# Three of 192 weight tiles brought as one transfer of 96 rows and four of 8 rows

## The chip, the cores and the metric

The kernel runs on one core of a Trainium2 chip. The metric is the device time of one execution in microseconds (us); the times given are medians of several runs.

## The reference

One layer of an encoder on 512 tokens of width 2048, float32: four token mixers with an input and an output projection, then a mixture of experts. What surrounds the change is the mixture: each token picks two of 32 experts, and each expert is a gated MLP.

```python
expert = grp[:, None] * EXPERTS_PER_GROUP + top_i        # 2 of 32 experts a token
a = jax.nn.silu(xblk @ w_gate[e]) * (xblk @ w_up[e])     # (2048 x 768) each
return a @ w_down[e]                                      # (768 x 2048)
```

The three weight matrices of 32 experts are 604 MB in float32. They are read once, and the kernel brings all of them whatever the routing is.

## The kernel before

The first 560 us or so are the mixers, the projections and the router. Then PE (TensorE) goes through the 32 experts, two at a time (`PAIRS`), each on up to 64 gathered token rows.

An expert's weights come as six tiles (`PARTS`) of 128 partitions x 24,576 bytes, 3072 KB each: two of `w_gate`, two of `w_up`, two of `w_down`. There are 192 tiles (`TILES`), numbered by `n`; tile `n` is part `n % 6` of expert `n // 6`, except at the very end, where `TAIL` changes the order. They go through a ring of five slots (and a sixth for the first round; `RING`, `slot_of`), in the regions `region_rest`, `region_h` and `region_w`. Every tile but the last two is one DMA issued by SP in `weight` (L392 for gate and up, L394 for down). Tiles 190 and 191 are cut into five pieces (`LAST`, L442).

The order of the transfers is SP's program order, one queue. In the loop over `n`, SP waits for `tile_used`, which PE raises when it is through with a tile, and issues the next tile into the slot that came free:

```python
for n in range(RING + 1, TILES):
    sp.wait_ge(tile_used, n - RING if n <= 2 * RING else n - RING + 1)
```

So four to five tiles are with the DMA engines at any time. PE waits in `landed(n)` (L1225 to L1228) for tile `n`'s semaphore to have counted 16 more, and then runs `gate_up` (matmuls of L1202) or `down` (L1220). For the last expert the down projections are L1163 and L1176, with L1152 adding the results into the tokens (L1141 for the experts before). Once in two experts POOL issues a gather of token rows (L549), which uses the DMA engines too. SP's queue carries nothing else in this part but the tiles (and `final_norm` once).

A tile's transfer of 128 rows runs on the core's 16 DMA engines, eight rows to each.

Of the kernel before, what the change touches and what calls it, by code (L numbers as in the profile page):

```python
# [30 lines left out]
P = 128  # L31
# [35 lines left out]
QK = KT // 2  # L67
DK = FT // 2
PARTS = 6
# [11 lines left out]

def added(c, t):
    return ADDS.index((c, t)) + 1


def nth_tile(n):
    return divmod(n, PARTS) if n < TILES - 2 * PARTS else TAIL[n - (TILES - 2 * PARTS)]
# [8 lines left out]
def build(nc, x, mix_norm, w_in, w_fourier, w_spatial, b_spatial, conv_w, w_pool, pool_scale, out_norm,  # L96
# [3 lines left out]
    with ctx:  # L100
        def sem(name):
            return ctx.enter_context(nc.semaphore(name))
# [98 lines left out]
        ring_gu = [r.rearrange("p (a b) -> p a b", a=QK) for r in ring]  # L201
# [45 lines left out]
        def slot_of(n):  # L247
            return n if n <= RING else (n - RING - 1) % RING
# [12 lines left out]
        wg_v = w_gate[0].rearrange("e (p k) n -> e p k n", k=KT)  # L261
# [14 lines left out]
        final_landed = sem("final_landed")  # L276
        tile_landed = [sem(f"tile_landed{s}") for s in range(RING + 1)]
        last_landed = [sem(f"last_landed{k}") for k in range(len(LAST))]
        last_down, last_hi, last_lo = sem("last_down"), sem("last_hi"), sem("last_lo")
        last_sum, last_added, f_redone, f_pre = sem("last_sum"), sem("last_added"), sem("f_redone"), sem("f_pre")  # L280
        over_landed = [sem(f"over_landed{s}") for s in range(PARTS)]
# [49 lines left out]
        def _(sp):  # L331
# [56 lines left out]
            def weight(expert, part, slot, landed):  # L388
                if part < 4:
                    src = (wg_v, wu_v)[part // 2]  # L390
                    q = part % 2
                    sp.dma_start(ring_gu[slot], src[expert, :, q * QK:(q + 1) * QK, :]).then_inc(landed, 16)  # L392
                else:
                    sp.dma_start(ring_down[slot], wdn_v[expert, part - 4]).then_inc(landed, 16)  # L394

            def tile(n):
                s = slot_of(n)
                weight(*nth_tile(n), s, tile_landed[s])

            def save_columns(n):  # L400
# [6 lines left out]
            for u in (37, 38):  # L407
                raw_unit(u)
            sp.wait_ge(y_normed, KT)
            tile(0)  # L410
            for u in (39, 40):
                raw_unit(u)
# [3 lines left out]
            save_columns(2)  # L416
            sp.wait_ge(w_ready, UNITS)
            tile(1)

            def save_last(t):  # L420
# [3 lines left out]
            for t in range(NT - 1):  # L424
                save_last(t)
            sp.wait_ge(w_used, UNITS)
            tile(2)
            save_last(NT - 1)
            tile(3)
# [45 lines left out]
        def _(pool):  # L475
# [94 lines left out]
            for t in range(NT):  # L570
                pool.wait_ge(last_added, added(0, t))
                g.tensor_tensor(gained[:, t, :], x_sb[:, t, 0:FINAL], final_row[:, 0:FINAL], ALU.mult).then_inc(f_gained, 1)
# [3 lines left out]
        def _(ae):  # L576
# [173 lines left out]
            for t in (0, 1):  # L750
                ae.wait_ge(last_added, added(0, t))
                square_first(t, f_pre, 2 * t + 1)
# [13 lines left out]
            def rms_last(t):  # L766
                ae.wait_ge(last_added, max(added(0, t), added(1, t)))
                if t < NT - 1:
                    src, junk_t, pre = x_sb[:, t, HALF:], junk3[3 + t], stat[:, 16 + t:17 + t]
                else:  # L770
                    src, junk_t, pre = x_sb[:, t, :], junk4, eps
                a.activation(junk_t, src, ACT.Square, accum_out=stat[:, t:t + 1]).then_inc(f_sq, 1)
                ae.wait_ge(f_sq, t + 1)
                a.activation(stat[:, NT + t:NT + t + 1], stat[:, t:t + 1], ACT.Sqrt, bias=pre, scale=1.0 / D).then_inc(f_rms, 1)
# [19 lines left out]
        def _(pe):  # L794
# [361 lines left out]
            def down_early():  # L1156
                for q in (0, 1):
                    slot = landed(TILES - 4 + q)
                    for kk in range(DK):
                        for c in (0, 1):  # L1160
                            for n in (0, 1):
                                j = 2 * c + n
                                mm = t_.matmul(ps[n * SLOTS:(n + 1) * SLOTS, 6 + c, :], aT[:, kk, q * SLOTS:(q + 1) * SLOTS],  # L1163
                                               ring_down[slot][:, kk, j * 512:(j + 1) * 512],
                                               start=(q == 0 and kk == 0), stop=(q == 1 and kk == DK - 1))
                    mm.then_inc(tile_used, 1)
# [58 lines left out]
            def landed(n):  # L1225
                s = slot_of(n)
                pe.wait_ge(tile_landed[s], 16 if n <= RING else 16 * ((n - 1) // RING + 1))
                return s  # L1228

            plan(0, True)  # L1230
# [2 lines left out]
            for e in range(E):  # L1233
                i, b = divmod(e, 2)
                n = e * PARTS if e < E - 1 else TILES - 8
                if e == E - 1:
                    pe.wait_ge(at_ready, e)
                for part in range(4):
                    if part < 2:
                        pe.wait_ge(hte_ready, 2 * e + part + 1)  # L1240
                    gate_up(part, landed(n + part))
                    if i and part in ((0, 1) if b else (1, 2)):
                        pe.wait_ge(hte_ready, 2 * e + 2)
                        combine(i - 1, 2 * b + (part if b else part - 1))
                if i:
                    pe.wait_ge(comb_added, 8 * (i - 1) + 4 * b + 4)
                if not b:
                    if i + 1 < PAIRS:
                        plan(i + 1)
                    transpose_rows(i, 1)  # L1250
                elif i + 1 < PAIRS:
                    transpose_rows(i + 1, 0)
                transpose_act(e)
                if e < E - 2:
                    pe.wait_ge(at_ready, e + 1)
                    if e:
                        pe.wait_ge(m_lo_ready, 2 * e)
                    for part in (4, 5):
                        down(b, part, landed(n + part))
# [574 lines left out]
```

## Time and profile before

| | |
|---|---|
| median of 3 runs | 2025.66 us (2024.97 to 2026.42) |
| the profiled execution, its own time | 2022.0 us |
| its span, first to last instruction | 2020.2 us |
| PE busy | 1854.8 us, 92% |
| DVE, POOL, ACT busy | 595.2, 249.6, 182.8 us |
| HBM read | 679.73 MB |

The page's slices are a fortieth of the span each, 50.5 us. A digit of the DMA line is the mean busy share of the 16 DMA engines in tenths; the line of GB/s is what they moved. In the chain that ended last, "DMA" is time in which PE waited, directly or through others, for a transfer to land, counted from its issue.

### The profile page before, as it was taken

The page shows a single profiled execution, that of the slowest core. Times are in us where ns is not written, and L with a number is a line of the kernel's source. Part 1 is how long each engine was busy: PE and PEld are TensorE (multiplying, and loading weights), DVE is VectorE, ACT ScalarE, POOL GpSimd, SP SyncE. Part 2 cuts the span into 40 slices and gives each one's busy share as a digit, 9 for nine tenths or more (in the row PEclk, how much of TensorE's full clock was granted, in tenths as well). Part 3 has the DMA queues.
Part 4 walks back from the last instruction along what each step waited for, and adds up shares of the span by engine and source line. Part 5 has one row for each costly group of instructions (what it writes and reads, how often), then busy time and mean ns, then how long its engine had stood idle before and what let it go on. Part 6 is the DMA issues. An engine that isn't in the chain of part 4 may idle for free.

```text
span 2020.2 us, 20896 instructions
## 1 busy us (share of the span) xinstructions
PE 1854.8 (92%) x9414; PEld 1056.3 (52%) x9414; DVE 595.2 (29%) x839; ACT 182.8 (9%) x274; POOL 249.6 (12%) x100
## 2 busy tenths in 40 slices
PE   8999999999969999899889989999898989888895
PEld 7887878788844444444344444444344444434342
DVE  3221656621142223122222223222222313222224
ACT  4000110101110010000000000000001000000003
POOL 4333535444200000000000000000000000000001
PEclk9999999999979999999999999999999999999998
DMA  7222233443389999999999999999999999999995
GB/s 275 84 78 84 64 103 90 175 171 113 115 343 424 429 430 429 429 429 429 430 430 430 429 430 430 429 429 428 432 428 431 429 428 429 429 430 429 429 427 205
DMA packets 68746, 681.12 MB, mean 337 GB/s; under 512 B 10352, under 2 KB 13616, under 8 KB 42416
## 3 DMA queue, kind: packets, MB, share of 16 engines
q1 hardware_dynamic: 65792, 671.16, 79.7%
q0 software_dynamic: 2304, 8.39, 1.0%
q8 instruction: 76, 1.25, 0.3%
q10 hardware_dynamic: 560, 0.21, 0.0%
q14 instruction: 14, 0.11, 0.0%
HBM read 679.73 MB, written 8.39 MB: 341 GB/s over the span
## 4 chain that ended last, share of the span: by engine, by line
PE 55%; DMA 43%; DVE 1%; issue 0%; ACT 0%; DVEq 0%; ACTq 0%
DMA region_rest<-in_w_gate 23%; PE banks L1202 19%; PE banks L814 15%; PE banks L1008 9%; DMA region_w<-in_w_gate 8%; DMA region_rest<-in_w_up 5%; DMA region_h<-in_w_gate 5%; PE banks L1141 3%; PE banks L1220 2%; DMA region_w<-in_w_down 1%; PE banks L892 1%; PE banks L904 1%; PE banks L841 1%; PE banks L1126 1%; PE banks L1176 1%; DMA region_h<-x_rows,region_rest 1%
## 5 line engine op out<-in xcount | busy, mean ns | idle before, releaser
L1202 PE MATMUL banks<-region_rest,region_w 128*64 128x384 f32 x2464 | 425.3, 499 | 58.8 <-DMA region_rest<-in_w_gate 43.8
L1202 PEld LDWEIGHTS banks<-region_rest,region_w 128*64 128x64 f32 x2464 | 185.7, 140 | 289.9 <-issue 219.7
L1658 DVE TENSOR_TENSOR region_x<-banks,region_x 128x1024 f32<-128x1024 f32 x120 | 141.4, 1220 | 587.7 <-PE banks L1141 587.7
L814 PE MATMUL banks<-split_h,split_w 128*128 128x512 f32 x864 | 273.7, 394 | 0.5 <-DVE split_w L1310 0.5
L494 POOL TENSOR_TENSOR split_w<-region_rest,split_w 128x2048 fp32r<-128x2048 f32 x42 | 196.9, 4688 | 302.8 <-DVE split_w L1317 302.8
L1220 PE MATMUL banks<-region_rest,region_w 128*64 128x512 f32 x864 | 213.0, 650 | 15.8 <-DVE region_w L1684 12.4
L814 PEld LDWEIGHTS banks<-split_h,split_w 128*128 128x128 f32 x864 | 162.2, 188 | 35.2 <-issue 0.7
L549 POOL DMA_INDIRECT region_h<-x_rows,region_rest x16 | 16.0, 1001 | 1271.2 <-PE banks L1126 1260.1
L814 PE MATMUL banks<-split_w 128*128 128x512 f32 x432 | 168.2, 389 | 0.0
L1008 PE MATMUL banks<-split_w,split_h 128*128 128x512 f32 x512 | 159.2, 392 | 0.0
L1202 PE MATMUL banks<-region_w 128*64 128x384 f32 x832 | 141.5, 493 | 18.8 <-DMA region_w<-in_w_gate 16.0
L1202 PE MATMUL banks<-region_h,region_w 128*64 128x384 f32 x800 | 136.0, 493 | 14.9 <-DMA region_h<-in_w_gate 9.5
L1220 PEld LDWEIGHTS banks<-region_rest,region_w 128*64 128x64 f32 x864 | 64.8, 149 | 150.8 <-issue 125.7
L1664 DVE TENSOR_TENSOR split_w<-banks,split_w 64x1024 fp32r<-64x1024 f32 x60 | 73.2, 1220 | 184.7 <-ACT split_w L709 183.8
L1141 PE MATMUL banks<-split_w 128*128 128x512 f32 x480 | 126.6, 406 | 0.0
L1317 DVE CAST split_w<-region_rest 128x2048 fp32r<-128x2048 f32 x43 | 53.2, 1237 | 210.0 <-PE banks L814 118.5
L1141 PEld LDWEIGHTS banks<-split_w 128*128 128x128 f32 x480 | 85.4, 188 | 51.6 <-issue 35.9
L1202 PEld LDWEIGHTS banks<-region_w 128*64 128x64 f32 x832 | 62.2, 138 | 94.9 <-issue 71.0
L1008 PEld LDWEIGHTS banks<-split_w,split_h 128*128 128x128 f32 x512 | 95.4, 188 | 22.5 <-issue 3.1
L1202 PEld LDWEIGHTS banks<-region_h,region_w 128*64 128x64 f32 x800 | 59.3, 138 | 88.8 <-issue 66.4
L715 ACT ACTIVATE region_w<-banks,region_rest 128x384 f32<-128x384 f32 x32 | 18.6, 582 | 902.9 <-PE banks L1202 902.9
L1008 PE MATMUL banks<-split_w 128*128 128x512 f32 x256 | 99.7, 389 | 0.0
(236 smaller groups left out, 1255.7 us busy)
## 6 DMA issues: line engine op xcount, KB each, us to landing
region_rest<-in_w_gate SPq DMA_DIRECT2D x39, 3072.0 KB, 31.7
region_rest<-in_w_up SPq DMA_DIRECT2D x38, 3072.0 KB, 30.4
region_rest<-in_w_down SPq DMA_DIRECT2D x36, 3072.0 KB, 30.8
region_h<-in_w_up SPq DMA_DIRECT2D x13, 3072.0 KB, 30.8
region_w<-in_w_up SPq DMA_DIRECT2D x13, 3072.0 KB, 30.2
region_w<-in_w_down SPq DMA_DIRECT2D x13, 3072.0 KB, 31.1
region_w<-in_w_gate SPq DMA_DIRECT2D x13, 3072.0 KB, 31.1
region_h<-in_w_down SPq DMA_DIRECT2D x13, 3072.0 KB, 31.3
```

The lines of the kernel that those rows point to most:

```text
L494: g.tensor_tensor(w_lo[u % 2], raw[u % RAW], w_hi[u % 2].bitcast(F32), ALU.subtract).then_inc(w_ready, 1)
L814: mm = t_.matmul(ps[:, 4 * (c % 2) + m, :], w[s][:, kk, cols_m], h[:, k, :], start=(k == 0 and w is w_hi and h is h_hi), stop=(k == KT - 1 ...
L841: mm = t_.matmul(ps[:, m, :], w[0][:, kk, m * P:(m + 1) * P], h[:, kk, :], start=(kk == 0 and w is w_hi and h is h_hi), stop=False)
L892: mm = t_.matmul(half, ab[:, s, h, c * HD:(c + 1) * HD], dft[:, c, s, :], start=(c == 0 and a == 0), stop=(c == 1 and a == 1))
L904: mm = t_.matmul(ps[:, m, :], wf[:, k, m * P:(m + 1) * P], fT[:, k, :], start=(k == 0), stop=(k == NH - 1))
L1008: mm = t_.matmul(ps[:, 4 * ((n + 1) % 2) + t, :], y[:, k, rows_t], w[s][:, kk, :], start=(k == 0 and y is y_hi and w is w_hi), stop=(k == ...
L1141: mm = t_.matmul(ps[:, 2 + 2 * c + n, :], back[c][:, t * P:(t + 1) * P], y[c][:, n * 512:(n + 1) * 512], start=(y is m_hi), stop=(y is m_lo))
L1202: mm = t_.matmul(ps[h * SLOTS:(h + 1) * SLOTS, u, 0:HF], hTe[:, k, :], ring_gu[slot][:, kk, h * HF:(h + 1) * HF], start=(k == 0), stop=(k ...
L1220: mm = t_.matmul(ps[g * SLOTS:(g + 1) * SLOTS, 6 + n, :], aT[:, kk, q * SLOTS:(q + 1) * SLOTS], ring_down[slot][:, kk, (2 * c + n) * 512:( ...
L1317: v.tensor_copy(w_hi[u % 2], raw[u % RAW]).then_inc(w_hi_ready, 1)
L1658: v.tensor_tensor(tile, ps[:, 2 + 2 * c:4 + 2 * c, :], tile, ALU.add).then_inc(comb_added, 1)
L1664: v.tensor_tensor(y_rows(m_lo, b, c), ps[g * SLOTS:(g + 1) * SLOTS, 6:8, :], y_rows(m_hi, b, c).bitcast(F32), ALU.subtract).then_inc(m_lo_ ...
```

## The change

```diff
+EVEN = (36, 96, 156)
...
+        rest_landed = sem("rest_landed")
...
             def tile(n):
                 s = slot_of(n)
+                if n in EVEN:
+                    sp.dma_start(ring_gu[s][0:96], wg_v[n // PARTS, 0:96, 0:QK, :]).then_inc(tile_landed[s], 16)
+                    for r in range(96, P, 8):
+                        sp.dma_start(ring_gu[s][r:r + 8], wg_v[n // PARTS, r:r + 8, 0:QK, :]).then_inc(rest_landed, 16)
+                    return
                 weight(*nth_tile(n), s, tile_landed[s])
...
             def landed(n):
                 s = slot_of(n)
                 pe.wait_ge(tile_landed[s], 16 if n <= RING else 16 * ((n - 1) // RING + 1))
+                if n in EVEN:
+                    pe.wait_ge(rest_landed, 64 * (EVEN.index(n) + 1))
                 return s
```

Tiles 36, 96 and 156 are the first gate tiles of experts 6, 16 and 26. In the changed kernel each is issued as five DMAs: rows 0 to 95 on the tile's own semaphore, then rows 96 to 103, 104 to 111, 112 to 119 and 120 to 127 on a semaphore of their own, for which PE also waits. The 96 rows are six rows for each of 16 engines. The transfers of eight rows are meant for eight of the engines, one row each, so that these eight have 6 + 4 = 10 rows of the tile and the other eight have six. The bytes, their source and their place in SBUF are the same.

SP's instructions at tile 36, before (the tile is the first of the two at the third row):

```order
L394 DMA region_rest<-in_w_down 128x6144 [waits tile_used]
L392 DMA region_rest<-in_w_gate 128x6144 [waits tile_used] x2
L392 DMA region_h<-in_w_up 128x6144 [waits tile_used]
```

and in the changed kernel, whose lines are numbered at least four higher:

```order
L398 DMA region_rest<-in_w_down 128x6144 [waits tile_used]
L403 DMA region_rest<-in_w_gate 96x6144 [waits tile_used]
L405 DMA region_rest<-in_w_gate 8x6144 x4
L396 DMA region_rest<-in_w_gate 128x6144 [waits tile_used]
L396 DMA region_h<-in_w_up 128x6144 [waits tile_used]
```

The one transfer has become five, with no wait between them; the order of the tiles has not moved. The rows at tiles 96 and 156 read alike.

## Rows read from the trace of the kernel before

**Rows 1.** The page: DMA busy tenths and GB/s in 40 slices.
```profile
DMA  7222233443389999999999999999999999999995
GB/s 275 84 78 84 64 103 90 175 171 113 115 343 424 429 430 429 429 429 429 430 430 430 429 430 430 429 429 428 432 428 431 429 428 429 429 430 429 429 427 205
```

**Rows 2.** Busy time by stretch (PE, PEld, DVE, ACT, POOL, PEclk, DMA share, GB/s).
```profile
700.00:800.00 100.00, 92.10 (x512) 43.32 (x510) 24.99 (x36) 5.24 (x6) 0.98 (x1) 1.00 1.00 429
1300.00:1400.00 100.00, 93.37 (x497) 44.07 (x493) 26.33 (x43) 5.24 (x6) 0.99 (x1) 0.95 1.01 430
1800.00:1900.00 100.00, 90.12 (x487) 42.45 (x485) 23.69 (x36) 5.24 (x6) 0.99 (x1) 0.97 1.00 429
```

**Rows 3.** Waits of PE, 600 to 1990 us (total us, times, longest).
```profile
PE banks L1202 <- DMA region_rest<-in_w_gate: 43.8, 24, 4.2
...
PE banks L1202 <- DMA region_w<-in_w_gate: 16.0, 9, 2.5
PE banks L1202 <- DMA region_rest<-in_w_up: 14.8, 11, 2.0
PE banks L1202 <- DMA region_h<-in_w_gate: 9.5, 7, 2.0
```

**Rows 4.** DMA issues by line: count, KB each, median us to landing.
```profile
region_rest<-in_w_gate SPq DMA_DIRECT2D x39, 3072.0 KB, 31.7
```

**Rows 5.** Timeline of SP, 792 to 812 us: the issue of tile 36 and the next.
```profile
801.40 8.23 SPq L392 DMA_DIRECT2D region_rest<-in_w_gate  x2
```

**Rows 6.** Timeline of PE at the first use of tiles 36 and 156.
```profile
833.55 7.08 PE L1202 MATMUL banks<-region_rest,region_w 128*64 128x384 f32 x32 [2.03 <-DMA region_rest<-in_w_gate]
...
1729.82 3.45 PE L1202 MATMUL banks<-region_rest,region_w 128*64 128x384 f32 x20 [2.03 <-DMA region_rest<-in_w_gate]
```

**Rows 7.** The chain that ended last, 1900 us to the end.
```profile
1946.32 29.73 DMA region_w<-in_w_down
1976.05 0.04 issue
1976.09 5.37 PE banks L1163 x24
1981.46 5.18 PE banks L1176 x23
...
1990.90 5.33 PE banks L1176 x24
```

**Rows 8.** Timeline of PE, 1969 to 1992 us.
```profile
1968.80 5.37 PE L1163 MATMUL banks<-region_h,region_w 128*64 128x512 f32 x24 [0.61 <-DMA region_h<-in_w_down]
1976.09 5.37 PE L1163 MATMUL banks<-region_w 128*64 128x512 f32 x24 [1.92 <-DMA region_w<-in_w_down]
```

**Rows 9.** Busy time by stretch at the end of the weights (columns as in rows 2).
```profile
1968.00:1976.00 8.00, 5.56 (x26) 1.96 (x24) 0.56 (x1) 0.00 (x0) 0.00 (x0) 1.00 1.00 411
1976.00:1980.00 4.00, 3.91 (x18) 1.35 (x20) 0.00 (x0) 0.00 (x0) 0.00 (x0) 1.00 0.94 358
1980.00:1984.00 4.00, 4.00 (x22) 1.42 (x20) 1.84 (x3) 2.15 (x4) 0.00 (x0) 1.00 0.58 237
1984.00:1988.00 4.00, 2.61 (x14) 0.59 (x10) 1.44 (x3) 1.18 (x2) 0.00 (x0) 1.00 0.51 209
1988.00:1992.00 4.00, 3.15 (x14) 1.91 (x16) 2.65 (x3) 0.70 (x1) 0.56 (x1) 1.00 0.23 92
```

**Rows 10.** DMA queues: packets, MB, share of 16 engines.
```profile
q1 hardware_dynamic: 65792, 671.16, 79.7%
q0 software_dynamic: 2304, 8.39, 1.0%
q8 instruction: 76, 1.25, 0.3%
```

## The prediction

> **What bounds the kernel now.** First the page's slices. From the thirteenth to the thirty-ninth, about 600 to 1970 us, the DMA digit is 9 and the rate stands at 424 to 432 GB/s [rows 1]. The stretches of 100 us say it more finely: DMA share 1.00, 429 or 430 GB/s, with PE busy 90 to 93% [rows 2]. So all 16 DMA engines work without a gap, and PE, though it looks full, waits for landings: 43.8 us on gate tiles in `region_rest` alone, never more than 4.2 us at once [rows 3]. A tile lands 31.7 us after its issue [rows 4], over four times the 7.33 us that its 3,145,728 bytes take at 429 GB/s, so the queue is four tiles deep and never runs dry.
>
> The time is then decided by the DMA engine that ends last. Every tile gives each of 16 engines eight rows of 24,576 bytes. One row takes an engine 7.33 / 8 = **0.917 us**; I call this a row time.
>
> Do all engines end together? They don't. The share is 1.00 until 1976, 0.94 until 1980, then 0.58, 0.51 and 0.23 in stretches of 4 us [rows 9]. A share near one half for 8 us is what it looks like when half of the engines have run out and the other half goes on. The bytes of these four stretches are 4 x (358 + 237 + 209 + 92) = 3584 KB; all engines together would need 8.4 us for them and be done at 1984.4 instead of about 1990.7. So the late half stands some 8 to 10 us behind the early half, the last engine of which stops at about 1983. Where the lag comes from is only partly seen: instruction fetches (76 packets) and gathers (8.39 MB) use the same engines and need not be even [rows 10].
>
> Last the chain at the end. PE waits for the down tile issued at 1946.32, which lands at 1976.05, and runs on from there to the end with short steps of DVE and ACT [rows 7]. This is tile 189. Two tiles follow it, 14.7 us of work for each engine, so the late half brought its share of tile 189 at 1976.05 and the slowest of the early half at about 1983 - 14.7 = **1968.3**.
>
> **The change part by part.** *SP* issues twelve DMAs more. Tile 36 is issued at 801.40 and used at 833.55 [rows 5, 6]; a fraction of a microsecond on SP is hidden by that queue, so I count nothing. If the queue were empty it would cost that fraction, three times. *PE* waits on a second semaphore; it already waits 2.03 us for tile 36 and for tile 156 [rows 6], so the check itself is free, and only when the rows land matters.
>
> *The rows moved.* Three tiles with two rows less for one half and two more for the other: 6 row times, 5.5 us. If that is all, and the relieved half is the late one, tile 189 is complete in the late half at 1976.05 - 5.5 = 1970.5 and in the early half at 1968.3 + 5.5 = 1973.8. The later counts: 2.2 us earlier than now. PE can take this up, since it waits 1.92 us there and 0.61 us one step before [rows 8]. This part is **-2.2 us**, not 5.5, because the early half has a slow engine of its own. Its best bound is -5.5.
>
> *What the eight-row transfers do to each other.* In a tile of 128 rows each engine brings eight rows, and the 16 reach 429 GB/s: each writes at its full 26.8 GB/s, to partitions that no other engine writes in that tile. In the new transfers eight engines each write one row at the same time into eight neighbouring partitions, 96 to 103, then 104 to 111, and so on. The trace has no heavy transfer of this kind. Bounds: if neighbours don't disturb each other, one of these transfers takes one row time and there is no cost. If all eight share one way in that is as fast as one engine, it takes eight row times. In between, four engines on one way make four row times. I take the four, for two reasons: the rate of 26.8 GB/s for an engine is also what the whole machine shows divided by 16, so I see no spare speed on the way in; and the middle of one and eight in ratio is near three to four. The Trainium skill, page SBUF — State Buffer, section "Door 1: The DMA port swizzle", speaks against the change here: four neighbouring partitions share one port, and a transfer to partitions 0 to 3 got 27.6 GB/s in all; no run here has shown it yet, and by this rule one transfer of eight rows takes four row times or five, since a port also has its usual engine.
>
> With four, the four transfers of a tile take 16 row times where four were meant: 12 too many. They come one behind the other on each engine, so nothing overlaps. If the engine that regularly writes into those partitions takes its turn as well (five on a way), it is 20 and 16 too many. I take **13**, near the lower end, because the eight engines don't arrive at the same moment, which gives a little back. Three tiles: 39 row times, 35.8 us, all in the early half. It cannot be made up later: the engines have no gap [rows 2]. Nor can PE's spare 10% help, since it spares PE, not the DMA.
>
> *Sum.* Tile 189 in the early half: 1968.3 + 5.5 + 35.8 = 2009.6, against 1976.05 now: **+33.5 us**. What comes after it on PE is unchanged. On the profiled execution 2022.0 + 33.5 = 2055.5. The median of the runs shown is 3.7 us above that execution, so I forecast 2025.7 + 33.5 = **2059**. With 12 row times too many it is 2056, with 16 it is 2067; allowing for more give and take, the forecast's own range is 2048 to 2070. What is late next is the early half: it turns into the late one at tile 36, by 10 us or more.
>
> **The rivals.** *No disturbance.* Each engine writes at its own speed wherever it writes. Then only -2.2 us is left: 2023.5, between 2020 and 2025.7. For it: 16 transfers side by side reach 429 GB/s without a gap [rows 2], so engines don't trouble each other at HBM, and the 11 us of difference that the moved rows make is about the lag. Against it: nothing in the trace has two engines at neighbouring partitions for long. This is the case on the other side, not slower; it decides if an eight-row transfer takes under about 1.5 row times. A measurement of this kernel can tell 0.2%, 4.1 us, so it would mostly read as no change.
>
> *Two on a way.* The way in has twice an engine's speed, so four engines take two row times: four too many a tile, 12 in all, 11.0 us; 1968.3 + 5.5 + 11.0 - 1976.05 = +8.7: 2034.
>
> *All eight on one way.* 28 too many a tile, 84 in all, 77 us: +74.8, 2100. I see little for it, since a full tile's rows are neighbours across engines too and run at full rate.
>
> *The wrong half.* No view names an engine. If the eight engines that get ten rows are the late ones, without disturbance, they end 5.5 us later: 2031. The page DMA: Bandwidth & Descriptors of the Trainium skill, section "Why a DMA increments its semaphore by 16 and not by 1", has such a transfer on the lowest-numbered engines; which half lags no row here shows.
>
> *It doesn't do what it says.* The eight rows are spread over all 16 engines after all: no shift of load, no crowding worth the name, 2025.7.
>
> **How the numbers follow.** Four or five on a way 0.52; two on a way 0.10; eight 0.04; no disturbance 0.26, of which 0.06 gains over 4.1 us (the early half's slow engine is less slow than I read it) and 0.20 not; wrong half 0.05; no effect 0.03. Slower by over 0.2%: 0.52 + 0.10 + 0.04 + 0.05 = 0.71. Within: 0.20 + 0.03 = 0.23. Faster: 0.06. No disturbance has over 2 in 10, so the range has to reach it: from 2022.5, which leaves out the larger gains, to 2070, above the 2067 of the highest of the main case. It leaves out some 0.15.
>
> **What the profile of the changed kernel would show.** If I am right: PE's wait for tiles 36, 96 and 156 grows from 2.03 us to over 10, and "longest" on `in_w_gate` with it. The GB/s fall clearly below 429 in some 15 us before each of these landings, while the DMA share stays at 1.00: engines that are held up count as busy. The transfers of eight rows take some 15 us longer than the 96 rows from issue to landing. The end of the weights still shows a step in the DMA share, now with the other half first, and longer. If no disturbance: 429 GB/s throughout, waits of 2 to 3 us at the three tiles, and in the last 15 us of weights a DMA share that falls from 1.00 to 0 within about 5 us. If the wrong half: the same rate, but the stretch of half share is 5 to 11 us longer. I am wrong altogether if the time rises while both the rate and the half-share stretch stay as they are; then it would be SP or PE, which I put at nothing.

## The result, and the profile after

The changed kernel takes 2089.3 us (median of 4 runs, 2081.1 to 2095.8) against 2025.3 us before: ratio 1.0317, 95% interval 1.0302 to 1.0333, slower by 64 us. The forecast was slower, 2059 us, in a range that ended at 2070. The sign and the three places were right; the size, 33.5 us, was half of what came. The profiled execution took 2087.4 us, its span is 2085.6.

The page of the changed kernel, its DMA lines in 40 slices (52.1 us each now):

```profile
DMA  7222133443499999999999999999999999999993
GB/s 266 81 94 78 66 101 95 173 162 121 171 389 424 431 427 387 367 429 429 430 429 430 429 430 327 389 432 428 429 431 429 429 429 301 374 427 429 430 414 127
```

Against [rows 1]: the digit stays at 9 from the thirteenth slice to the thirty-ninth, the rate does not stay. It dips in three places (387 and 367, 327 and 389, 301 and 374), where tiles 36, 96 and 156 are in transfer. Elsewhere it stands at 424 to 432 as before, up to the thirty-ninth slice (414). The DMA engines are busy all through and move less.

The first of the three places in steps of 5 us (columns as in rows 2):

```profile
815.00:820.00 5.00, 4.55 (x33) 2.98 (x29) 1.03 (x2) 0.00 (x0) 0.00 (x0) 1.00 0.98 416
820.00:825.00 5.00, 4.80 (x24) 1.64 (x24) 1.34 (x3) 0.00 (x0) 0.00 (x0) 1.00 1.10 369
825.00:830.00 5.00, 1.47 (x6) 0.29 (x4) 0.00 (x0) 0.00 (x0) 0.00 (x0) 0.81 1.03 236
830.00:835.00 5.00, 5.00 (x14) 1.42 (x12) 0.00 (x0) 0.00 (x0) 0.00 (x0) 0.50 1.09 182
835.00:840.00 5.00, 2.36 (x12) 0.56 (x8) 1.50 (x2) 2.04 (x2) 0.00 (x0) 1.00 1.00 147
840.00:845.00 5.00, 0.00 (x0) 0.00 (x0) 0.94 (x1) 0.00 (x0) 0.00 (x0) 0.68 0.88 157
845.00:850.00 5.00, 2.13 (x8) 1.05 (x10) 0.00 (x0) 0.00 (x0) 0.00 (x0) 0.50 0.94 383
```

The DMA share stays near 1.00 while the rate falls to 147 GB/s. Against 429 these seven stretches lack 13 + 60 + 193 + 247 + 282 + 272 + 46 GB/s over 5 us each, 5565 KB, which is 13.0 us of transfer at the full rate. The trouble begins at 820 us, before the eight-row transfers run: tile 36 comes behind four others in the queue, its 96 rows come first, and the first of its eight-row pieces on any engine lands at 834.6 us. Most of the loss comes later, though: by the same view 315 GB/s from 815 to 833 us, 4.8 us lost, and 223 GB/s from 833 to 850 us, 8.2 us lost.

PE's waits, 600 to 2060 us, and its timeline at tile 36:

```profile
PE banks L1211 <- DMA region_rest<-in_w_gate: 66.3, 23, 10.6
PE banks L1229 <- DMA region_rest<-in_w_down: 26.1, 6, 10.9
```
```profile
829.10 8.26 PE L1229 MATMUL banks<-region_rest,region_w 128*64 128x512 f32 x24 [3.54 <-DMA region_rest<-in_w_down]
847.87 12.58 PE L1211 MATMUL banks<-region_rest,region_w 128*64 128x384 f32 x64 [10.51 <-DMA region_rest<-in_w_gate]
```

The first use of tile 36 is at 847.87 instead of 833.55 [rows 6], after a wait of 10.51 us. The tile before it, which the change doesn't touch, is also late (PE waits 3.54 us for it at L1229, the same matmuls as L1220 before). The longest wait for such a down tile, 10.9 us, comes at tile 96, again for the tile before the cut one. So the cut tile holds up its neighbours.

The end of the weights (columns as in rows 2), and the chain that ended last there:

```profile
2028.00:2032.00 4.00, 3.33 (x18) 1.41 (x18) 0.56 (x1) 0.00 (x0) 0.00 (x0) 1.00 0.90 370
2032.00:2036.00 4.00, 2.20 (x12) 0.55 (x7) 0.00 (x0) 0.00 (x0) 0.00 (x0) 1.00 0.35 137
2036.00:2040.00 4.00, 2.49 (x6) 0.77 (x8) 0.00 (x0) 0.00 (x0) 0.00 (x0) 0.56 0.94 322
2040.00:2044.00 4.00, 4.00 (x14) 1.23 (x12) 0.00 (x0) 0.00 (x0) 0.00 (x0) 0.59 0.34 137
2044.00:2048.00 4.00, 4.00 (x22) 1.26 (x18) 1.57 (x3) 2.15 (x4) 0.00 (x0) 1.00 0.12 48
2048.00:2052.00 4.00, 2.88 (x14) 0.70 (x10) 1.46 (x3) 1.05 (x2) 0.00 (x0) 1.00 0.06 26
```
```profile
2006.32 31.14 DMA region_w<-in_w_down
2037.46 0.04 issue
2037.51 8.22 PE banks L1172 x24
2045.72 5.18 PE banks L1185 x23
```

The step near one half for 8 us [rows 9] is gone. In its place most engines run dry by 2036, since SP's issue of the fourth of the five last pieces takes 14.0 us and that of the fifth begins only at 2035.7 (the reason is not shown), and one or two of 16 go on to 2052 (shares 0.12 and 0.06). Tile 189 lands at 2037.46 instead of 1976.05 [rows 7]: **61.4 us** later. From there to the end of the span it takes 48.1 us, before 44.2 us: **4.0 us** more, since PE had stood idle and its granted clock was 0.56 and 0.59 in these stretches, near the lower of its two levels, 1.2 of 2.4 GHz: the 24 matmuls of L1172 took 8.22 us instead of 5.37 (L1163 before), and after a second idle time, at 0.69, the 8 of L1161 took 3.40 instead of 2.06 (L1152 before). Together 65.4 us, the growth of the span.

The trace also holds each engine's own increment of a tile's semaphore. When the first and the last of the 16 engines had brought their share of a tile, in us, and how much later the last was than before:

```
tile      before            changed kernel        last engine
38        843.8 to  848.0    856.3 to  862.1       +14.0
98       1288.7 to 1296.0   1317.8 to 1331.0       +35.0
159      1741.2 to 1751.6   1792.6 to 1812.5       +60.9
189      1963.4 to 1976.0   2017.3 to 2037.5       +61.4
```

14, 21 and 26 us for the three cut tiles and next to nothing in between. The first engine is late nearly as much: 12.5, 29.2, 51.4 and 54.0 us. That the early half alone would be held up was wrong from the first tile on: all 16 are. Before, the 16 increments of tile 189 stand in two groups, eight from 1963.4 to 1968.1 and eight from 1974.2 to 1976.0, which bears out the two halves of the prediction. In the changed kernel 14 stand from 2017.3 to 2026.6 and the last two at 2033.0 and 2037.5: two engines decide the landing. The semaphore of the eight-row transfers also shows that they run on eight engines: each of the 12 has eight increments at its landing and one lump for the rest at its issue.

### The profile page after: what moved, and what is told of

It is laid out like the page before. It is cut to its first block, busy times and chain, and to the rows that moved or that the text cites. A ratio compares the mean times of both kernels' runs of the same rounds, so it can differ in the third digit from the quotient of the medians.

```text
span 2085.6 us, 20908 instructions
## 1 busy us (share of the span) xinstructions
PE 1864.3 (89%) x9414; PEld 1057.5 (51%) x9414; DVE 594.9 (29%) x839; ACT 182.8 (9%) x274; POOL 249.7 (12%) x100
## 4 chain that ended last, share of the span: by engine, by line
PE 52%; DMA 45%; another core or an unknown queue 1%; DVE 1%; issue 0%; ACT 0%; SPq 0%; DVEq 0%; ACTq 0%
DMA region_rest<-in_w_gate 23%; PE banks L1211 18%; PE banks L823 14%; DMA region_w<-in_w_gate 9%; PE banks L1017 8%; DMA region_h<-in_w_gate 6%; DMA region_rest<-in_w_down 4%; PE banks L1150 3%; PE banks L1229 2%; DMA region_w<-in_w_down 1%; PE banks L901 1%; PE banks L913 1%; PE banks L850 1%; PE banks L1185 1%; DMA region_h<-x_rows,region_rest 0%
## 5 line engine op out<-in xcount | busy, mean ns | idle before, releaser
L1229 PE MATMUL banks<-region_rest,region_w 128*64 128x512 f32 x864 | 215.8, 657 | 38.5 <-DMA region_rest<-in_w_down 26.1
L1229 PEld LDWEIGHTS banks<-region_rest,region_w 128*64 128x64 f32 x864 | 65.0, 150 | 176.0 <-issue 126.8
```

The source lines that it names most:

```text
L1229: mm = t_.matmul(ps[g * SLOTS:(g + 1) * SLOTS, 6 + n, :], aT[:, kk, q * SLOTS:(q + 1) * SLOTS], ring_down[slot][:, kk, (2 * c + n) * 512:( ...
```

## The experiments

Ratios are to the kernel before on the same chip, with the 95% interval; microseconds are the ratio's excess times the 2024 to 2025 us of the kernel before. Only the three tiles are changed in each, and PE's wait for the second semaphore is set to the number of transfers.

### Is it the 96 rows or the eights?

```diff
 a1_96_32: rows 96 to 127 as one transfer (16 engines, two rows each)
+    sp.dma_start(ring_gu[s][0:96], wg_v[n // PARTS, 0:96, 0:QK, :]).then_inc(tile_landed[s], 16)
+    sp.dma_start(ring_gu[s][96:128], wg_v[n // PARTS, 96:128, 0:QK, :]).then_inc(rest_landed, 16)
 a2_spread_high: the eight rows of a transfer lie four partitions apart
+    for r in range(96, 100): ... ring_gu[s][r:P:4] ...
 a3_spread_low: rows 32 to 127 at once, rows 0 to 31 by eights, four apart
+    for r in range(4): ... ring_gu[s][r:32:4] ...
 a4_neighbours_low: rows 32 to 127 at once, rows 0 to 31 by neighbouring eights
+    for r in range(0, 32, 8): ... ring_gu[s][r:r + 8] ...
```

> Tiles 36, 96, 156 as rows 0 to 95 and one transfer of rows 96 to 127 (16 engines, two rows each). The changed kernel measured +64 us, 21 us a tile. Theory 1, crowding in the eight-row transfers: here two engines write into each group of four neighbouring partitions instead of four, two rows each, so 2 to 4 row times of 0.917 us too many a tile: +5 to +11 us, ratio 1.003 to 1.006. Theory 2, the 96-row transfer costs by itself (six rows an engine don't fall on partitions that no other engine writes): most of the cost stays, +45 to +65 us, ratio 1.022 to 1.032.

> Rows 0 to 95, then four transfers of eight rows whose partitions lie four apart (96, 100, ... 124; then 97, 101, ...), one engine to each group of four partitions. Theory 1: each group has this engine and the one that regularly writes there, so 4 rows take up to 8 row times, 4 too many a tile: 0 to +11 us, ratio 1.000 to 1.006. Theory 2: +45 to +65 us, ratio 1.022 to 1.032.

> The 96 rows are rows 32 to 127, and the four transfers of eight rows take partitions 0, 4, ... 28, then 1, 5, ... 29 and so on, so that each of the eight engines would write where it does in a full tile. Theory 1: no crowding at all, -2 us to +2 us, ratio 0.998 to 1.001. Theory 2: +45 to +65 us, ratio 1.022 to 1.032.

> The control of the one before: rows 32 to 127, and rows 0 to 31 as four transfers of eight neighbouring rows. Theory 1: crowding as in the changed kernel, now in the partitions that the eight engines themselves write in full tiles: +40 to +65 us, ratio 1.020 to 1.032. Theory 2: +45 to +65 us as well. If it is far cheaper than the changed kernel, what costs is writing into the other half's partitions, which neither theory has.

| | ratio | us |
|---|---|---|
| changed kernel | 1.0317 (1.0302 to 1.0333) | +64 |
| a1, 96 + 32 | 1.0238 (1.0214 to 1.0262) | +48 |
| a2, eights four apart, other half | 1.0294 (1.0277 to 1.0311) | +60 |
| a3, eights four apart, partitions 0 to 31 | 1.0211 (1.0193 to 1.0229) | +43 |
| a4, neighbouring eights, partitions 0 to 31 | 1.0291 (1.0272 to 1.0311) | +59 |

Theory 1, which the prediction rests on, has the cost in the eight-row transfers alone. It gave a3 no cost at all and falls with its +43 us. Theory 2 is nearer: some two thirds of the cost are there whatever is done with the other 32 rows, though a3 came 2 us below its range. What the eights do on top depends on their partitions: four apart in partitions 0 to 31 they cost least, as neighbours in the same partitions 16 us more (a4 against a3), and four apart in partitions 96 to 127 17 us more (a2 against a3, where the place of the 96 rows changes too). The crowding of neighbours that I forecast shows in a4 against a3. In the partitions of the changed kernel it doesn't: there the eights cost 60 us four apart (a2) and 64 as neighbours, and the intervals overlap.

At tile 36 the two parts can be told apart in time. From 815 to 833 us, with the 96 rows under way, a3 moved 303 GB/s, a4 303 and the changed kernel 315. From 833 to 850 us, with the eights (and the last of the 96 rows on the engines that are behind), a3 moved 348, a4 250, a2 228 and the changed kernel 223. No run has the 96 rows beside a rest that is known to be free, so 43 us is the most that they can be given, not a measurement of them alone.

### Without a 96-row transfer

From here on theory A is that a group of neighbouring partitions has one way in, as fast as one engine, and that engines which meet there share it; theory B is a fixed cost of each transfer.

```diff
 in all three: 128 rows of 18,432 bytes, then the other 6,144 bytes of each row
+    sp.dma_start(ring_gu[s][:, 0:6, :], wg_v[n // PARTS, :, 0:6, :]).then_inc(tile_landed[s], 16)
 c2_columns: in one transfer of 128 rows
+    sp.dma_start(ring_gu[s][:, 6:8, :], wg_v[n // PARTS, :, 6:8, :]).then_inc(rest_landed, 16)
 c1_columns_spread: in 16 transfers of eight rows, four apart
+    for base in range(0, P, 32):
+        for r in range(base, base + 4): ... ring_gu[s][r:base + 32:4, 6:8, :] ...
 c3_columns_neighbours: in 16 transfers of eight neighbouring rows
+    for r in range(0, P, 8): ... ring_gu[s][r:r + 8, 6:8, :] ...
 d1_64_64: whole rows, in two transfers
+    ... ring_gu[s][0:64] ...
+    ... ring_gu[s][64:128] ...
```

> The three tiles cut by columns instead of rows: 128 rows of 18,432 bytes, then 128 rows of the other 6,144 bytes, both on all 16 engines. The runs so far put 44 us on the 96-row transfer and 16 to 20 us on the eight-row ones. Theory A, paths: a group of partitions has one way in, as fast as one engine, and only a transfer of all 128 rows gives each engine a way of its own. Then this costs nothing: ratio 0.999 to 1.001. Theory B, a cut tile costs because it is several transfers with their own fixed cost: +5 to +40 us, ratio 1.003 to 1.02.

> The same 128-row transfer of 18,432 bytes a row, then the other 6,144 bytes of every row in 16 transfers of eight rows whose partitions lie four apart, so that eight engines have ten rows' worth and the other eight six, as in the changed kernel, without a 96-row transfer. Theory A: the early half writes two rows' worth into ways that the late half also uses, so both go at half speed for a while and the late half is not relieved: -1 to +8 us, ratio 0.9995 to 1.004. If only an engine's own load counted: -2 us, and a gain of up to 5.5 us, ratio 0.997 to 0.999. Theory B: 16 times a fixed cost, over +20 us, ratio above 1.01.

> As the one before, but the 16 transfers are of eight neighbouring rows each, as the changed kernel has them. Load by engine, bytes and number of transfers are the same as in the one before. Theory A: four or more engines on a way make four rows' worth take 16: 12 row times too many a tile at most, +15 to +33 us, ratio 1.0075 to 1.0165. Theory B: the same as the one before.

> The three tiles as rows 0 to 63 and rows 64 to 127, each on 16 engines with four rows each, in equal shares. Theory A: each transfer reaches only half of the ways, two engines on each, so eight rows' worth take 16 row times: 7.3 us a tile and somewhat more by the mismatch with the full tiles beside it, +20 to +50 us, ratio 1.010 to 1.025. If what costs in the 96-row transfer were its number of rows or the uneven load: near 0, ratio below 1.003.

| | ratio | us |
|---|---|---|
| c2, by columns | 0.9997 (0.9987 to 1.0006) | -1 |
| c1, 10 : 6 by columns, four apart | 1.0088 (1.0072 to 1.0105) | +18 |
| c3, 10 : 6 by columns, neighbours | 1.0100 (1.0083 to 1.0117) | +20 |
| d1, 64 + 64 | 1.0209 (1.0192 to 1.0226) | +42 |

c2 clears the second transfer, its semaphore and PE's wait: they cost nothing. Theory B, a fixed cost of 5 us or more, falls with it. A small one, 0.4 us for each of 48 transfers, would still give the 18 to 20 us of c1 and c3, but their traces speak against it: at every moment from 820 to 860 us at least 16 packets were under way, so a wait between transfers left no gap, and it is the packets that got longer. The 6,144-byte pieces of tile 36 took 0.23 to 0.25 us in c2. In c1, 53 of 128 took under 0.26 us and 69 took 0.40 to 0.49; at tile 156 it is 64 of 128 under 0.26. The short ones mostly come first, and partitions 0 to 63 are issued first. So eights four apart seem to be free there and to take twice the time in partitions 64 to 127; no record names the partition of a packet. d1 has two transfers with equal load for all 16 engines and costs as much as a 96-row one, so the uneven load is not what costs either. Its stretch of 40 us around tile 36, and that of c2:

```profile
815.00:855.00 40.00, 27.18 (x129) 11.22 (x127) 4.82 (x6) 2.04 (x2) 0.00 (x0) 0.83 1.00 311
```
```profile
815.00:855.00 40.00, 35.80 (x187) 16.57 (x184) 7.17 (x8) 2.62 (x3) 0.00 (x0) 0.96 1.01 430
```

311 GB/s instead of 430 lacks 40 x 119 / 430 = 11.1 us of transfer. By theory A two engines on each way would make 7.3 us, eight row times too many; the rest would be lost by the full tiles beside it.

c1 is the cleanest way of giving one half ten rows' worth and the other six: the full-tile pattern for three quarters of the bytes, one engine to a group of four for the rest. It too is slower, by 18 us, twice as much as theory A allowed. Neighbours in place of spread eights (c3) add 2 us, within the intervals; my theory had at least 7 us more for them. Four engines on one way would make pieces of 0.95 us, and the longest piece of c3 at tile 36 took 0.53: up to about twice the time of c2, never four times.

### One cut tile at a time

```diff
-EVEN = (36, 96, 156)
 b1_tile_36
+EVEN = (36,)
 b2_tile_156
+EVEN = (156,)
```

> The changed kernel with tile 36 alone cut (96 rows and four times 8). In the changed kernel's profile the landings were 14 us later after tile 36, 21 us more after tile 96 and 26 us more after tile 156. Both theories: +12 to +16 us here, less what the lead of the early half hides at the end, ratio 1.004 to 1.008.

> The changed kernel with tile 156 alone cut. Theory S, the cost of a cut tile depends on how far the two halves of engines are apart when it comes (2 us at tile 36, 8 to 9 us at tile 156), since then the cut tile of one half meets full tiles of the other: +20 to +28 us, ratio 1.010 to 1.014. Theory R, each cut tile scatters the engines and makes the next one dearer: as for tile 36, +12 to +16 us, ratio 1.006 to 1.008.

b1: ratio 1.0089 (1.0072 to 1.0106), +18 us. b2: 1.0109 (1.0091 to 1.0127), +22 us. In the profiles the last engine is 16.1 us late after tile 36 in b1, where it was 14.0 in the changed kernel, whose instructions are the same up to there; so one profile can differ from another by 2 us at one tile. It is 19.8 us late after tile 156 in b2, where it was 26 us more in the changed kernel. b1 lies above the range of both theories, b2 in that of theory S. Neither theory is shown: 156 alone is dearer than 36 by 4 us, within the intervals, and cheaper than after two others by some 6 us in one profile each. No run has tile 96 alone, so whether the three costs add up is open; 18 + 22 would leave 24 for it.

### Partitions near each other, or HBM rows near each other?

```diff
 g1_every_second: alternate partitions from the same alternate rows
+    ... ring_gu[s][0:P:2], wg_v[n // PARTS, 0:P:2, 0:QK, :] ...
+    ... ring_gu[s][1:P:2], wg_v[n // PARTS, 1:P:2, 0:QK, :] ...
 h1_halves_from_alternate
+    ... ring_gu[s][0:64], wg_v[n // PARTS, 0:P:2, 0:QK, :] ...
+    ... ring_gu[s][64:P], wg_v[n // PARTS, 1:P:2, 0:QK, :] ...
 h2_alternate_from_halves
+    ... ring_gu[s][0:P:2], wg_v[n // PARTS, 0:64, 0:QK, :] ...
+    ... ring_gu[s][1:P:2], wg_v[n // PARTS, 64:P, 0:QK, :] ...
```

> The three tiles as partitions 0, 2, 4, ... 126 and partitions 1, 3, ... 127, two transfers of 64 rows on 16 engines with four rows each, equal load. The cut into rows 0 to 63 and 64 to 127 cost +42 us. If that cost came from each transfer reaching only one half of the partitions, this one reaches all of them and is free: ratio 0.999 to 1.002. Theory A, it counts who writes where: engines take their rows in order (engine 0 has partitions 0, 2, 4, 6), so two engines still meet on the same groups of partitions and on those of a full tile's engines, and the cost stays, +30 to +50 us, ratio 1.015 to 1.025.

> The cut into partitions 0 to 63 and 64 to 127 (+42 us), but with the source rows taken alternately (0, 2, 4, ... into the first, 1, 3, 5, ... into the second), as in the cut that was free. The three gate tiles thus hold rows in another order, which changes the output. Theory D, the destination decides (engines meet on partitions in SBUF): +35 to +50 us, ratio 1.017 to 1.025. Theory Q, the source decides (64 neighbouring rows of HBM against rows spread over the tile's whole stretch): free, ratio 0.999 to 1.002.

> The mirror image: partitions 0, 2, ... 126 and 1, 3, ... 127 as destination, source rows 0 to 63 and 64 to 127; again the three gate tiles hold their rows in another order. Theory D: free, ratio 0.999 to 1.002. Theory Q: +35 to +50 us, ratio 1.017 to 1.025.

| partitions written | rows read | | ratio | us |
|---|---|---|---|---|
| 0 to 63, 64 to 127 | the same | d1 | 1.0209 (1.0192 to 1.0226) | +42 |
| every second | the same | g1 | 0.9998 (0.9988 to 1.0007) | 0 |
| 0 to 63, 64 to 127 | every second | h1 | 1.0216 (1.0199 to 1.0234) | +44 |
| every second | 0 to 63, 64 to 127 | h2 | 1.0000 (0.9991 to 1.0010) | 0 |

The partitions written decide, the rows read don't. This is the plainest result of the study, and g1 is the one that spoke against me: I had expected +30 to +50 us, because I took it that engines get a transfer's rows in order. They can't, or not with the ways as I drew them. In the stretch around tile 36, h1 and then h2:

```profile
815.00:855.00 40.00, 27.61 (x127) 11.31 (x125) 4.82 (x6) 2.04 (x2) 0.00 (x0) 0.83 1.01 315
```
```profile
815.00:855.00 40.00, 34.64 (x192) 16.02 (x189) 7.17 (x8) 2.62 (x3) 0.00 (x0) 1.00 1.00 430
```

The same share of busy engines, 315 against 430 GB/s.

The single packets show how much they are held up. A row of 24,576 bytes is one packet; these are the packets that began from 800 to 880 us, counted in the traces by their duration:

```
                        up to 0.96 us  to 1.5  to 2.0  to 3.0  longer   longest
before                       1363         3       0       0       0     1.42 us
g1 every second              1364         3       0       0       0     1.42
h2 every second              1364         3       0       0       0     1.42
d1 64 + 64                    999        27     184       0       0     1.94
h1 64 + 64                   1000        28     183       0       0     1.94
a1 96 + 32                    998        31     153      26       0     2.79
a2 96, eights high spread     997        20     144      36       0     2.89
a3 96, eights low spread     1056        37     127      14       0     2.44
a4 96, eights low neighbours  959        41     110      67       0     2.87
changed kernel                974        34      95      62       7     3.25
```

In d1 and h1 the long packets of this stretch take twice the usual 0.91 us and never three times it, as if two engines shared what one has alone in a full tile. With eights of neighbours there are many near three times, and some above. These engines are held up while they count as busy, and the packets of full tiles beside the cut one are among them: d1 has 184 of 1.5 to 2.0 us, while its cut tile has 128 packets.

In time the picture is sharper. In d1 every one of the 158 packets that began from 824 to 842 us took 1.68 to 1.94 us. In the changed kernel all 59 that began from 824 to 830 us, with the 96 rows under way, took 1.6 to 1.9 us, and 56 of the 57 from 833 to 842 us, with the eights under way, took 2.5 to 3.25. Not one ran at the usual speed, so all 16 engines are held up at once. Why it takes them all is open.

## Why the prediction was half right

*What bounds the kernel.* Right. Up to the last pieces the DMA engines did not have a gap, and what they lost was lost for good: the last engine's delay grew at each cut tile and did not shrink between them. SP and PE's second wait cost nothing (c2), as I had it.

*The rows moved, -2.2 us.* Not shown. No run gave the shift without the disturbance; the one with least of it, c1, is 18 us slower. That c1 doesn't win fits the picture that the late half's partitions take their bytes at one engine's speed whoever brings them, so that moving rows to other engines relieves nobody; it is argued, not shown. Which half was late no run shows.

*What the eight-row transfers do, +35.8 us.* Right in part. With the eights of the changed kernel packets take 2.5 to 3.25 us, three row times or so, and neighbours cost more than spread ones in partitions 0 to 31 (a4 against a3, 16 us for three tiles). But in partitions 96 to 127 eights four apart, which by my picture meet one other engine and not three or four, cost nearly as much (a2), so that neighbours crowd one way is not shown to be the cause there. The size was too large, 35.8 for 16 (a4 less a3) to 21 (changed kernel less a3). Four row times for each transfer is a bound that they keep below; why is not shown. I had the eights land 15 us after the 96 rows; at the three tiles their last share landed 5.0, 6.7 and 6.6 us after the last of the 96.

*The step that failed* is in the sum, 1968.3 + 5.5 + 35.8: its only disturbance is that of the eight-row transfers. The 96-row transfer stands in it at nothing, without a reason. The runs showed a large cost in its place: +43 us of 64 are left in a3, whose eights, four apart in partitions 0 to 31, are of the kind that seem to run at full speed in c1. So it is probably the larger part; no run measures it alone. I had argued from the full tile that each engine writes "to partitions that no other engine writes in that tile", and did not ask if this still holds with six rows an engine. With four neighbouring ones it costs 42 us (d1), and the long packets of the 96-row phase, 1.6 to 1.9 us for 0.91, are those of d1. A rival in which every transfer that is not a full tile meets the tiles beside it was missing from my list, and the range ended where the missing term began.

*Who is held up.* I had "all in the early half". After the first cut tile the 16 increments of tile 38, taken in order, are 12.5 to 14.6 us later than before, and those of tile 189 47 to 61 us. So there was no lead of the early half to hide 8 us of the loss, as my sum had it. That full tiles before and behind the cut one are slow because they share its partitions is argued, not shown.

*After the last landing.* I had "unchanged"; it was 4.0 us more, by PE's granted clock of 0.56 to 0.69 after its waits.

Counted together: 33.5 forecast for the landing of tile 189, 61.4 measured. My sum was 5.5 + 35.8 less 7.8 of lead. Without the lead and without the 5.5 that no run shows, and with 43 for the 96 rows and 16 to 21 for the eights, it would be 59 to 64. The terms were taken from the same runs that they explain, so that they add up is no proof of each.

*The rule of the Trainium skill.* The Trainium skill, page SBUF — State Buffer, section "Door 1: The DMA port swizzle", has partitions 0 to 63 reach 8 of 16 ports and so go at half the rate. The trace agrees: in d1 the packets take 1.5 to 1.94 us for 0.91. It also implies what I had not drawn from it, that a transfer need not be small to be slow. The same page of the Trainium skill, section "Can I just issue two DMAs to hit both halves?", says that only one transfer spanning all 128 partitions reaches all ports; g1 and h2, two transfers of 64 alternate partitions each, moved 430 GB/s, so here the measurement decides against that sentence.

## What to carry to other kernels

When DMA engines are the bound, cut a transfer by columns, or by alternate partitions, and not into blocks of neighbouring partitions: here a cut by columns or by every second partition was free, and three cuts of a 3 MB tile into 64 + 64 or 96 + 32 partitions cost 42 to 48 us, paid by the tiles beside it as well. Read the rate and the busy share together, since engines that wait for each other count as busy. And when you price a change that splits one operation in five, price the largest of the five as well as the odd ones.

## What the runs showed of the hardware

- Two transfers over 64 neighbouring partitions each ran at 311 GB/s in a stretch where two over every second partition ran at 430, with the same bytes and a DMA busy share of 1.00 in both (d1, h2). Of the partitions written and the HBM rows read, only the partitions matter (d1, g1, h1, h2).
- Engines can't both get a transfer's rows in order and meet on ways of four partitions, since g1 would then not be free. Which of the two is wrong, and how 96 rows are dealt out, stays open; no view names an engine.
- A transfer that is slow in this way slows full transfers beside it: PE waited 3.5 us for the tile before tile 36 and 10.9 us for the one before tile 96.
- The four runs of the changed kernel scatter over 15 us (2081 to 2096), those of the kernel before over 2 us beside them and up to 5 us in the later groups. How hard engines meet seems to depend on how far apart they are when the cut tile comes; this is argued from the scatter alone.
